# Moving a triangular inverse's block transfers to ScalarE's queue, with new placements for its steps, a changed tail order and one more tile on GpSimd

## The reference

```python
def _layer(x, w_in, ...):                      # x (1, 2048, 1024), w_in (1024, 3336)
    h = einsum('btd,dc->btc', x, w_in)         # q, k, v, z, b, a (group A), q, k, v, z (group B)
    ya = _deltanet_group(qa, ka, va, za, ba, aa, ...)  # 4 heads of 128, chunks, causal conv of 4
    yb = _swa_group(qb, kb, vb, zb, sinks)     # 8 query heads of 64, 2 kv heads, window 128
    y = einsum('btc,cd->btd', concatenate([ya, yb]), w_out)
    return layernorm(2 ** 0.25 * x + y, ln_g, ln_b)

# in _gated_delta_rule, for each chunk of tokens
a_mat = where(strict, (k_beta @ k.T) * decay, 0)
t_mat = inverse(eye + a_mat)                   # unit lower triangular
u, w = t_mat @ (v * beta), t_mat @ (k_beta * exp(g))
v_new = u - w @ s                              # state s goes from chunk to chunk
o = q_dec @ s + qk @ v_new
s = s * g_tot + k_dec.T @ v_new
```

## Time and profile before

| | |
|---|---|
| three runs | 1094.55, 1095.97, 1099.94 us; median 1095.97 |
| the profiled execution | 1094.55 us, its span 1092.8 us |
| granted clock of TensorE | 0.998 of 2.4 GHz |
| busy: PE, DVE, ACT, POOL | 1064.3, 690.1, 533.1, 116.1 us |
| first matmul wait at the start | 8.0 us |

### The profile page before, as it was taken

One profiled execution on the slowest core, in us unless ns is written; L12 is line 12 of the kernel. 1 busy time (PEld: TensorE's weight loads), 2 busy tenths in 40 slices (PEclk: granted clock), 3 DMA queues, 4 the chain that ended last, 5 costly groups with the idle time before them and its releaser, 6 DMA issues.

```text
span 1092.8 us, 19497 instructions
## 1 busy us (share of the span) xinstructions
PE 1064.3 (97%) x7212; PEld 846.6 (77%) x7212; DVE 690.1 (63%) x2079; ACT 533.1 (49%) x1557; POOL 116.1 (11%) x152
## 2 busy tenths in 40 slices
PE   7999999999999999999999999999999999999997
PEld 5877777768778787786887878787787878787785
DVE  5285859585655748567365674757537575758564
ACT  4556666654735444373363635435345645464300
POOL 3513132133200000011000000002000000002210
PEclk9999999999999999999999999999999999999999
DMA  8967475665562726263453461815354343612332
GB/s 276 315 212 260 156 280 189 247 202 165 203 223 80 250 75 226 76 211 100 165 196 134 140 236 42 268 51 184 116 187 163 126 157 127 226 63 80 117 116 77
DMA packets 58286, 183.55 MB, mean 168 GB/s; under 512 B 8464, under 2 KB 21200, under 8 KB 44880
## 3 DMA queue, kind: packets, MB, share of 16 engines
q1 hardware_dynamic: 58048, 182.05, 48.4%
q10 hardware_dynamic: 144, 0.26, 0.1%
HBM read 138.22 MB, written 44.07 MB: 167 GB/s over the span
## 4 chain that ended last, share of the span: by engine, by line
PE 63%; DVE 7%; DMA 2%; issue 1%; ACT 0%; SPq 0%; DVEq 0%
PE bank L843 33%; PE bank L894 9%; PE bank L1131 4%; PE bank L951 2%; PE bank L984 2%; PE bank L966 2%; PE bank L1101 1%; PE bank L1114 1%; PE bank L1111 1%; DVE y_cols L1783 1%; PE bank L1115 1%; PE bank L1024 1%; PE bank L1039 1%; DVE y_step L1779 1%; PE bank L1109 1%
## 5 line engine op out<-in xcount | busy, mean ns | idle before, releaser
L843 PE MATMUL bank<-xr,w 128*128 128x512 f32 x2496 | 654.3, 405 | 8.4 <-DVE xr L1525 8.0
L843 PEld LDWEIGHTS bank<-xr,w 128*128 128x128 f32 x2496 | 449.8, 189 | 102.9 <-issue 10.4
L894 PE MATMUL bank<-wo,y_split 128*128 128x512 f32 x432 | 114.3, 403 | 0.0
L894 PEld LDWEIGHTS bank<-wo,y_split 128*128 128x128 f32 x432 | 77.0, 189 | 14.5 <-issue 0.7
L1573 DVE SCALAR_TENSOR_TENSOR kq<-conv_in,convw_all,kq 128x512 f32<-128x512 f32 x96 | 76.9, 801 | 7.9 <-ACT conv_in L1185 5.9
L1476 ACT ACTIVATE o_scaled<-bank 128x128 f32<-128x128 f32 x64 | 17.7, 277 | 126.5 <-PE bank L1115 126.3
L1347 ACT ACTIVATE score<-score,neg_max 128x256 f32<-128x256 f32 (+1 forms) x128 | 62.7, 492 | 26.8 <-DVE neg_max L1745 26.8
L1906 DVE TENSOR_SCALAR steps<-bank,nb_rk 128x128 f32<-128x128 f32 x64 | 22.2, 347 | 63.0 <-PE bank L1111 63.0
L1909 DVE SCALAR_TENSOR_TENSOR state<-state,cols_all,bank 128x128 f32<-128x128 f32 x64 | 22.2, 347 | 61.9 <-PE bank L1114 61.9
L1779 DVE TENSOR_TENSOR y_step<-blocks,y_cols 128x60 f32<-128x60 f32 (+14 forms) x240 | 50.1, 209 | 9.3 <-DMA blocks<-n_spill 0.5
L777 POOL TENSOR_TENSOR xr<-y_tile,xr 128x256 fp32r<-128x256 f32 x8 | 6.0, 776 | 455.8 <-ACT xr L1166 455.8
(11 more groups left out here) (217 smaller groups left out, 1629.9 us busy)
## 6 DMA issues: line engine op xcount, KB each, us to landing
w<-w_split SPq DMA_DIRECT2D x78, 1024.0 KB, 5.6
w_split<-w SPq DMA_DIRECT2D x26, 1024.0 KB, 5.3
blocks<-n_spill SPq DMA_DIRECT2D x32, 256.0 KB
y_spill<-y_out SPq DMA_DIRECT2D x30, 256.0 KB, 5.7
x_tile<-w_in SPq DMA_DIRECT2D x13, 512.0 KB, 5.9
y_tile<-w_in SPq DMA_DIRECT2D x12, 512.0 KB, 6.4
y_tile<-y_spill SPq DMA_DIRECT2D x12, 512.0 KB, 6.2
x_tile<-x SPq DMA_DIRECT2D x12, 512.0 KB, 3.9
```

Of the source, the lines that this page charges most:

```text
L843: ins = nc.tensor.matmul(bank[JOBS[at].bank][:], w[:, turn % 3, wp, k, :], xr[:, xp, k], start=(step == 0), stop=(step == 3 * KT - 1))
L894: ins = nc.tensor.matmul(bank[JOBS[at].bank][:], y_place(t)[:, yp, k], wo[:, k, wp, half * UNIT:(half + 1) * UNIT], start=(step == 0), sto ...
```

## The change

Five parts.

1. `POOL_TILES` ends one tile later, so that tile 11 of the tail gets its gain and shift on POOL.
2. `Places` has new fractions for slots 0 to 2 (`first_unit`) and for slot 3, which now takes the values of a long slot. In long slots (3, 7, 11, 15) `first` is 0.4. Slots 4 to 6, 8 to 10 and 12 to 14 keep theirs.
3. `store_blocks` and `load_blocks` go from SP's program to ACT's. The store stands behind the squares of L1399 (in slot 3 behind the third x split), and the loads stand behind the exps of the first half's weights (in slot 3 behind `rq2`), with the same waits except the one for ACT's own squares.
4. In the last slot SP's order of `load_y`, `store_tile` and `load_x_tile` changes.
5. DVE emits the follow-ups due before `at.chunk(c)` at the head of each chunk step.

```diff
-POOL_TILES = range(8, 11)
+POOL_TILES = range(8, 12)
...
-        last_of_first = n == AH - 1
-        first = 0.56 if first_unit else 0.515 if short else 0.42 if last_of_first else 0.406 if long else 0.463
-        level = 0.034 if first_unit else 0.03 if short else 0.028
+        first = 0.55 if first_unit else 0.515 if short else 0.4 if long else 0.463
+        level = 0.03 if short else 0.028
         self.p16, self.y16, self.p32, self.y32, self.p64 = (first + level * a for a in range(5))
-        self.step0, self.step = (0.745, 0.0635) if first_unit else (0.7, 0.074) if short else (0.615, 0.093) if last_of_first else (0.6, 0.096) if long else (0.63, 0.09)
+        self.step0, self.step = (0.725, 0.069) if first_unit else (0.7, 0.074) if short else (0.6, 0.096) if long else (0.63, 0.09)
...
-            def store_blocks(n):
-                after(sp, picked, n, 2)
-                sp.dma_start(n_spill[n], y_step[:].rearrange("p t c -> p (t c)")).then_inc(n_stored.sem, 16)
-
-            def load_blocks(n):
-                after(sp, n_stored, n, 16)
-                after(sp, sq_done, n, 2 * CH)
...
-                store_blocks(n)
-                load_blocks(n)
                 if i < AH - 1:
                     after(sp, pt_ready, n, 2)
                     load_decay(n + 1)
...
                     load_y(12)
-                    load_y(13)
                     store_tile(8)
                     load_x_tile(10)
-                    load_y(14)
+                    load_y(13)
                     store_tile(9)
                     load_x_tile(11)
+                    load_y(14)
                     store_tile(10)
...
+            def store_blocks(n):
+                after(act, picked, n, 2)
+                act.dma_start(n_spill[n], y_step[:].rearrange("p t c -> p (t c)")).then_inc(n_stored.sem, 16)
+
+            def load_blocks(n):
+                after(act, n_stored, n, 16)
+                rows = n_spill[n].rearrange("(g b a) m -> b g (a m)", b=2, a=BASE // 2)
+                size = CH * BASE * BASE // 2
+                for b in range(2):
+                    source = rows[b].unsqueeze(1).to_broadcast([P // BASE, BASE, size])
+                    act.dma_start(shared[:, b * size:(b + 1) * size], source).then_inc(blocks_in[b].sem, 16)
...
                     for k2 in range(3):
                         x_hi(1, k2)
+                    store_blocks(n)
...
+                if n != AH - 1:
+                    store_blocks(n)
                 after(act, sq_done, n, 2 * CH)
...
                 if n == AH - 1:
+                    load_blocks(n)
                     after_jobs(n, 0.12)
                 weights(n, 0)
+                if n != AH - 1:
+                    load_blocks(n)
                 split_weight()
...
                 for c in range(CH):
                     one = slice(c, c + 1)
+                    after_jobs(n, at.chunk(c))
                     if c == 0:
                         gate_b(n, 1)
```

## The result

The changed kernel took 1107.02 us in the median of four runs (1106.35 to 1107.54), beside 1096.51 of the kernel before; the ratio is 1.0086, with a 95% interval of 1.0065 to 1.0106. All 13 of its executions on record lie between 1104.01 and 1109.13 us. It is slower by some 9.5 us by the ratio and by 10.5 by the two medians, where 3.2 were forecast, and the time lies outside the range of 1094 to 1104. More runs of the kernel before, made beside the experiments, have a median of 1097.6 to 1097.9 us, so its profiled execution (1094.55) was one of its fastest, 3 us under that median.

A forecast was written before the change was run, and what follows sets the result against it. The kernel was taken as bound by PE, busy 97%. Terms of 2.1 + 0.2 + 0.5 + 0 + 0.4 gave +3.2 on the median 1095.97, rounded 1099.0 us; range 1094 to 1104.

The forecast's parts named there:

- the blocks' landing: Blocks' loads on ACT's queue: earlier landing gains nothing, with little chance of less than nothing; 0 taken for the move.
- ACT held by the issue, 0: Issuing the blocks' DMAs from ACT's queue hides under its exps, 1.23 us fitting into a 1.6 us lead: 0.
- rival (1): ACT stands for the whole issue, making DVE late in slots 0 to 2: +2.4 on the sum, 1101.6; chance 0.22.
- Slots 0 to 2, +2.1: New fractions bring PE earlier to L1061 and L966, where it waits longer: 0.70 us a slot, +2.1 in all.
- Slots 3 and 4, +0.2: New slot 3 fractions: longer waits at L1061 and L966 against waits saved at L1111 and in slot 4; -1.3 to +2.3.
- POOL's collision ahead of L966: In slot 3, POOL's weight piece meets DVE's divide and `slopes` ahead of L966: +1.2, between 0 and 2.2.
- The q_in wait: Slot 4's 0.9 us wait for q_in hangs on work now started earlier; 0.5 us of it given back.
- Slots 7 and 11, +0.5: One dense step fewer ahead of L1061, where PE already waits 0.66 and 0.64: 2 x 0.23, +0.5.
- The tail, +0.4: Slot 15's new SP order and earlier DVE follow-ups: gains and losses together +0.4, from -0.6 to +2.7.
- the first two: Slot 15: x 10 landing earlier, -1.25; tile 10's second half ahead of the third resid, +1.2.
- the one for y 14: Slot 15: y 14's load, issued about 4.3 us later, delays the last resid: +0.6, between 0 and +2.9.
- Tile 11's 0: Tile 11 on POOL in the tail: its store and x 13's load some 3 us later, costing 0, up to +1.

The follow-up runs named there:

- e1: Kernel before with only the blocks' stores and loads moved to ACT's queue: 1100.84 us, ratio 1.003.
- e8: Kernel before with only slot 3's new fractions: 1095.72 us, ratio 0.9984.
- e2: Changed kernel with the blocks' stores and loads back on SP's queue, all else kept: 1102.23 us, ratio 1.0043.
- e5: As e1, with SP in slots 12 to 14 also waiting for both halves of the blocks before sending what follows: 1101.57 us, ratio 1.0034.
- e10: e9 with the blocks' transfers of slots 7 and 11 alone on ACT's queue: 1095.32 us, ratio 0.9979 to the kernel before.
- e4: Kernel before with only the new fractions for slots 0 to 2: 1101.15 us, ratio 1.0026.
- e7: Kernel before with only tile 11 of the tail put on POOL: 1099.15 us, ratio 1.001.
- e11: e9 with slot 3's `first` back at 0.42, its chunk-step fractions kept new: 1095.64 us, ratio 0.9989 to the kernel before.
- e6: Kernel before with only SP's new last-slot order and DVE's follow-ups at the head of each chunk step: 1099.94 us, ratio 1.0009.
- e3: Changed kernel with the blocks' transfers back on SP's queue from slot 12 on only: 1101.54 us, ratio 1.0029.
- e9: e8 with tile 8's store and x 10's load ahead of y 13 in the last slot: 1096.31 us, ratio 0.9988 to the kernel before.

## Why the prediction was wrong

**The step that failed: the blocks' landing.** The prediction weighed only what issuing costs ACT, and of the landing it said "Blocks landing earlier gain nothing", with 0.02 and 0.03 us in slots 12 and 14. It took for granted, without a reason, that on another queue they could not land later. In the kernel before the loads stood ahead of the decay rows, y and the weights in SP's queue; on ACT's queue they share the DMA engines with all of these. That makes the second half 2.6 to 3.2 us later in use (e1 against before, slots 12 and 13), in slots with no slack, and the trace of before showed which these were. Taken as 0, the term measured 3.2 alone (e1; its interval reaches from 1.6 to 4.8) and 4.8 in the full change (1107.0 - 1102.2; 4.7 by the two ratios, each known to about 2 us); in the profiles, slots 12 to 14 are 5.6 longer in e1 and 6.8 in the full change. That slack of 0.02 should have been a rival with the sign turned. In slot 12 it was not even slack: DVE had waited 0.53 us for the blocks before they landed.

**ACT held by the issue, 0:** right. Slots 0 to 2 of e1 are unchanged, and rival (1) is out (the prediction once calls it the second). ACT does stand for up to 0.8 us in slots 12 to 14, at no cost that shows.

**Slots 0 to 2, +2.1:** 1.9 to 2.1, right. It gives nothing back.

**Slots 3 and 4, +0.2:** 0.0 in the first pair of profiles, but by other parts. The wait at L1061 rose by 0.73 (0.76 had been said), and the 0.61 at L1111 went. The +1.2 for POOL's collision ahead of L966 did not come; a wait of 0.38 for a copy of ACT at L1077 came instead, and the clock fell for some 3 us behind the wait of 2.76. The q_in wait went in full. That the sum came out at 0.0 is luck, as slot 4 scatters by 5 us. By e8 these fractions are worth between a gain of 3.7 us and a loss of 0.1 (0.9966 to 1.0001).

**Slots 7 and 11, +0.5:** -0.1 and 0.0. The waits fell to 0.54 and 0.52 instead of rising. The placement by itself did what was said: with the blocks on SP (e2) they rose to 0.87 and 0.89, by 0.2 each. The move took that back, a coupling of two parts of the change that the prediction didn't have. In e1, without a new placement, these slots are 0.5 shorter each: POOL's low part of x (L777) ends 0.4 us into DVE's base case instead of 1.1 (in slot 7, 494.69 against a start at 494.32, and 494.67 against 493.53), and the first half of the base case takes 4.15 us instead of 4.67. That the shorter meeting with POOL makes this is read from the trace; no run separates it. With the blocks on ACT's queue slot 7 has the same length within 0.1 us in three profiles of the old placement (78.2 in e1, e5 and e10), where it is 78.4 to 79.6 with SP; four of the eight profiles with SP (e4, e7, e8, e11) have a wait of PE for POOL's part of x in slot 7 or 11, and none of the five with ACT.

**The tail, +0.4:** too low. Of the three terms the first two held (-1.1 and +1.0 in waits, for -1.25 and +1.2), and the one for y 14 was 0.6 to 1.1 for 0.6, with the forgotten 0.81 us of DVE in it; order and added calls alone gave +1.27 (e6). Tile 11's 0 was 0.3 alone (e7), though its wait was 0.7 to 0.9, near the upper bound that the prediction had named. Together +2.2 against +0.4, of which 0.6 to 0.8 are gone with the blocks on SP (e2, e3).

**The footing.** The sum was set on a median of three, 1095.97, and the later one of 30 executions is 1.7 higher. That alone moves 1099.2 to 1100.9; the blocks (4.8) and the tail (1.8) cover the rest of the distance to 1107. What is left open: why slots 12 to 14 cost 5.6 in the profile of e1 and only 3.2 in its median, what adds 0.6 to 0.8 to slot 15 in the full change, and how much of the difference between the full change and the sum of its parts is the clock.

## What to carry to other kernels

A transfer that is moved to another engine's queue leaves its place in line: what it stood ahead of now competes with it, so ask of each of its landings what slack it had, and of a landing with none what the larger transfers behind it will do to it. A gain from an earlier fetch and a loss from a later one often sit in the same reordering, and one run with half of the moves tells them apart. Where a wait on an engine is set by another's busy chain, taking work from ahead of it only lengthens it.

## What the hardware showed

The granted clock fell to 0.50 or 0.51, the 1.2 GHz level, behind some waits of TensorE, and not behind others as long. In slot 3 PE waited 2.58 us at L1061 in both e8 and e10. Of the five profiles with a wait of 2.58 or 2.59 there, it fell in three (e2, e3, e10) and not in two (e8, e9), and of the five with 2.02 to 2.04 it fell in one (e4). The windows behind it in e8, and then in e10:

```profile
236.00:239.00 3.00, 0.82 (x36) 1.00 0.71 244
239.00:242.00 3.00, 3.00 (x48) 1.00 0.26 45
```

```profile
236.00:239.00 3.00, 1.44 (x40) 1.00 0.47 160
239.00:242.00 3.00, 3.00 (x9) 0.51 0.23 44
```

Slot 3 was 70.19 us long in the one and 71.70 in the other: the fall costs 1.5 us. Over a whole execution it goes with a good part of the scatter. Of 94 executions of the kernel before, the 19 with a mean clock of 0.998 or 0.999 took 1096.5 us in the mean, the 18 with 0.995 took 1099.9, and the single one with 0.993 took 1103.6; by a straight line through all of them the clock accounts for some two fifths of the variance.
